# Eight gather slots instead of seven in a fused retention, convolution and expert layer

## The reference

```python
h = rmsnorm(x, g_mix)
q, k, v, g, gb, gc, hc = split(h @ w_in)
o = rms_scale(retention(state, rotary(q), rotary(k), v)) * silu(g)
conv_y, conv_new = short_conv(buf, gc * hc, conv_w)      # y = w0*e[t] + w1*e[t+1] + w2*e[t+2]
x = x + concat([o, gb * conv_y]) @ w_out
# peer(n(x)): per row and head
q = (n(x) @ wq).reshape(T, 8, 2, 128)
v1, i1 = top_k(q[:, :, 0] @ keys1.T, 16);  v2, i2 = top_k(q[:, :, 1] @ keys2.T, 16)
cand = v1[..., :, None] + v2[..., None, :]               # 256 pairs a head
top_s, sel = top_k(cand, 16);  eidx = (i1 * 128 + i2)[sel];  gate = softmax(top_s)
act = gelu(einsum('td,thkd->thk', n(x), u_tab[eidx]))
x = x + einsum('thk,thkd->td', gate * act, v_tab[eidx])
y = rmsnorm(x, g_fin)
```

## Time and profile before

| | |
|---|---|
| median of 3 runs | 3036.95 us (3034.13 to 3040.64) |
| the profiled execution | 3032.31 us, of it the span from first to last instruction 3030.5 us |
| busy shares | PE 75%, DVE 68%, ACT 67%, POOL 41% |
| gathers (software queue) | 1107.36 MB, packet time 88.6% of 16 engines' span |
| other loads and stores (hardware queue) | 116.88 MB, 9.7% |
| HBM traffic | 404 GB/s over the span |

### The profile page before, as it was taken

One profiled execution on the slowest core, in us unless ns is written; L12 is line 12 of the kernel. 1 busy time (PEld: TensorE's weight loads), 2 busy tenths in 40 slices (PEclk: granted clock), 3 DMA queues, 4 the chain that ended last, 5 costly groups with the idle time before them and its releaser, 6 DMA issues.

```text
span 3030.5 us, 36672 instructions
## 1 busy us (share of the span) xinstructions
PE 2286.4 (75%) x12800; PEld 1866.0 (62%) x12800; DVE 2071.6 (68%) x5121; ACT 2024.2 (67%) x3688; POOL 1238.6 (41%) x1060
## 2 busy tenths in 40 slices
PE   9976887787668878876667787888777676666766
PEld 7765776665557766755556665665656555555555
DVE  2467887566688775656888744566588899954454
ACT  1277666668677666686677766667767777676666
POOL 0133433334333333444433444434444444455653
PEclk9988999998888898988988989989878987666666
DMA  7599999999999999999999999999999999999997
GB/s 301 184 421 410 407 410 418 419 420 412 420 421 405 416 420 416 420 407 420 420 417 404 404 419 419 419 417 409 413 420 418 420 412 413 413 419 414 421 420 330
DMA packets 180569, 1226.65 MB, mean 405 GB/s; under 512 B 20736, under 2 KB 21952, under 8 KB 40736
## 3 DMA queue, kind: packets, MB, share of 16 engines
q0 software_dynamic: 152064, 1107.36, 88.6%
q1 hardware_dynamic: 28032, 116.88, 9.7%
q10 hardware_dynamic: 288, 0.07, 0.0%
HBM read 1219.37 MB, written 4.86 MB: 404 GB/s over the span
## 4 chain that ended last, share of the span: by engine, by line
DMA 37%; DVE 23%; PE 22%; ACT 12%; issue 6%; POOL 1%; DVEq 0%; ACTq 0%; POOLq 0%
DMA ring<-in_uv,idx 37%; DVE ring L1467 11%; PE expert_sum L1120 9%; ACT ring L877 5%; PE mm L918 4%; PE mm L927 2%; PE mm L1042 2%; ACT weights L873 2%; PE x_ps L980 2%; DVE pairs_left L1314 1%; ACT dots L864 1%; ACT L864 1%; DVE pairs_left L1402 1%; PE expert_sum L918 1%; POOL ring L662 1%
## 5 line engine op out<-in xcount | busy, mean ns | idle before, releaser
L662 POOL DMA_INDIRECT ring<-in_uv,idx x1056 | 1238.3, 1173 | 1768.3 <-PE expert_sum L1120 1553.9
L1120 PE MATMUL expert_sum<-ident_sb,ring 128*128 128x128 f32 x8448 | 1358.9, 315 | 590.2 <-ACT ring L877 588.5
L1467 DVE CUSTOM_DVE_ANT_0 ring<-ring,xn 128x1024 f32<-128x1024 f32 x1056 | 1286.2, 1222 | 738.1 <-DMA ring<-in_uv,idx 730.5
L1120 PEld LDWEIGHTS expert_sum<-ident_sb,ring 128*128 128x128 f32 x8448 | 1140.5, 163 | 848.3 <-ACT ring L877 781.8
L877 ACT ACTIVATE ring<-ring,weights 128x1024 f32<-128x1024 f32 x1056 | 1213.0, 1149 | 34.4
L864 ACT ACTIVATE dots<-dots 128x1 f32<-128x1 f32 x1056 | 211.6, 200 | 791.2 <-DVE dots L1467 789.2
L873 ACT ACTIVATE weights<-dots,gate 128x1 f32<-128x1 f32 x1056 | 311.1, 295 | 38.1
L918 PE MATMUL mm<-stream,xn_in 128*128 128x256 f32 (+1 forms) x912 | 253.7, 416 | 77.1 <-ACT qkvg L709 61.7
L1042 PE MATMUL mm<-turn,stream 128*128 128x256 f32 (+2 forms) x1024 | 274.1, 396 | 2.8 <-DVE xn_in L1159 2.8
L918 PEld LDWEIGHTS mm<-stream,xn_in 128*128 128x128 f32 (+1 forms) x912 | 164.4, 196 | 116.8 <-ACT qkvg L709 70.5
L927 PE MATMUL mm<-xn_in,stream 128*128 128x256 f32 (+1 forms) x640 | 184.8, 428 | 36.2 <-ACT conv_tmp L700 23.5
(11 more groups left out here) (235 smaller groups left out, 1521.1 us busy)
## 6 DMA issues: line engine op xcount, KB each, us to landing
stream<-in_wq SPq DMA_DIRECT2D x36, 1024.0 KB, 11.8
stream<-in_w_ret SPq DMA_DIRECT2D x26, 1024.0 KB, 9.5
stream<-in_w_conv SPq DMA_DIRECT2D x24, 1024.0 KB, 12.1
ring<-in_uv,idx POOLq DMA_INDIRECT x1056, 12.4
ring<-in_w_ret SPq DMA_DIRECT2D x7, 1024.0 KB, 12.5
x<-in_x SPq DMA_DIRECT2D x8, 512.0 KB, 9.8
w_out_sb<-in_w_out SPq DMA_DIRECT2D x1, 4096.0 KB, 29.1
out_y<-xn SPq DMA_DIRECT2D x8, 512.0 KB, 12.1
```

The source lines that it names most:

```text
L662: pool.indirect_dma_start(ring[:, g % RING, :], None, uv, bass.IndirectOffsetOnAxis(ap=rows, axis=0)).then_inc(landed[g % RING], 16)
L1120: ins = pe.matmul(expert_sum[:, c * P:(c + 1) * P], ring[:, g % RING, D + c * P:D + (c + 1) * P], ident_sb[:, :], is_transpose=True, start ...
L1467: dve.tensor_tensor_reduce(u, u, xn[:, t % 3, :], 1.0, 0.0, ALU.mult, ALU.add, dots[:, g % RING:g % RING + 1]).then_inc(dotted, 1)
```

## The change

- `RING` is 8. All eight blocks of the first group's retention weights are loaded into the ring, and the eighth's two loads into `stream` go. `BUFFERS` stays 3.
- The space for it: `pairs_left` goes. The pairs and the one-hot table stand in `scores`. `best16` replaces in place, with a wait more between FIND_INDEX8 and MATCH_REPLACE8. The one-hot table is made in two halves of 256 with three instructions each.
- ACT's copy of the next scores waits for the whole choice before it (`chosen`) instead of for the last read of the scores.
- `conv_tmp` shrinks to `taps`; the C projection and the filter's result stand in `conv_out`.
- `idx` and `gate` have three places instead of four; from t = 3 on a choice waits until tile t-3's gathers have been weighed.
- `state_s` is `qT`. The sample's state is loaded later and stored earlier, the last group's first query copy waits for that store, and the last group's three tiles take Silu on ACT in place of Tanh on ACT and a multiplication on DVE.
- The rotary table stands in the unused tail of `turn` (for t = 1, of `xn_in`).

```diff
-RING = 7
+RING = 8
...
-    + [(USES[0][use_at(0, "ret", RING, t)][3], 0, "ret", 0, t) for t in GROUPS[0]]
...
-        conv_out = sb("conv_out", [P, CH, wide])
-        conv_tmp = sb("conv_tmp", [P, 2, wide + 4])
+        conv_out = sb("conv_out", [P, CH, wide + 2])
+        taps = sb("taps", [P, wide + 4])
...
-        pairs_left = sb("pairs_left", [P, 2, 2 * NK])
...
-        idx = sb("idx", [P, 4, STEPS], I32)
-        gate = sb("gate", [P, 4, STEPS])
+        idx = sb("idx", [P, 3, STEPS], I32)
+        gate = sb("gate", [P, 3, STEPS])
...
-        state_s = sb("state_s", [P, H, P])
+        state_s = qT[:, :].rearrange("p (h c) -> p h c", h=H)
...
+        hot = scores[:, :, :].rearrange("p s k -> p (s k)")
+        pairs = hot.rearrange("p (i j) -> p i j", i=TOPK)
+        left = xn[:, 2, 0:2 * NK]
...
-                yield base_of(1) + STEPS
-                sp.wait_ge(rotated, 2)
-                sp.dma_start(state_s[:, :, :], ret_state).then_inc(state_in, 16)
+                yield mix_at(SAMPLE) - 20
+                sp.wait_ge(keyed, scores_before(mix_at(SAMPLE)) - 1)
+                sp.dma_start(state_s, ret_state).then_inc(state_in, 16)
...
+            def store_sample_state():
+                yield mix_at(SAMPLE) + 20
+                sp.wait_ge(gated, RANK[SAMPLE] + 1)
+                sp.dma_start(out_ret_s, state_s).then_inc(sample_state_out, 16)
...
                     if kind == "C":
-                        if unit:
-                            act.wait_ge(dve_took, taken(j, q - 1)[1])
-                        act.activation(gate_c[:, 0:width(j)], bank[:, 0:width(j)], ACT.Copy).then_inc(act_took, 1)
+                        wait(act, x1_ready, GROUPS[j][0])
+                        act.activation(conv_out[:, unit // 3, 0:width(j)], bank[:, 0:width(j)], ACT.Copy).then_inc(act_took, 1)
...
+                if j == len(GROUPS) - 1:
+                    g = vg_of(t)[0:n, RET:]
+                    act.activation(g, g, ACT.Silu).then_inc(silu_done, 1)
+                else:
...
+                    if j == len(GROUPS) - 1:
+                        act.wait_ge(sample_state_out, 16)
...
                     if t < SAMPLE:
-                        wait(act, scores_read, pick(h, t) - 1)
+                        act.wait_ge(chosen, pick(h, t))
...
-            def best16(values, indices, s, rest, read=None):
+            def best16(values, indices, s):
                 op(dve.max(values[:, 0:8], s))
                 settle()
                 op(dve.max_index(indices[:, 0:8], values[:, 0:8], s))
...
+                settle()
+                op(dve.match_replace(s, values[:, 0:8], s, LOWEST))
+                settle()
+                op(dve.max(values[:, 8:16], s))
...
                             if s == 0:
                                 dve.wait_ge(keyed_copied, c)
+                                if t > 2:
+                                    dve.wait_ge(weighed, end_of(t - 3))
...
+                        for e in range(2):
+                            part = slice(e * TOPK // 2, (e + 1) * TOPK // 2)
+                            op(dve.tensor_tensor(hot3, bc(iota_sb[0:n, :], 1, TOPK),
+                                                 bc(half_f[0:n, part, :].rearrange("p k s -> p (k s)"), 2, TOPK),
+                                                 ALU.is_equal))
+                            settle()
+                            if e == 0:
+                                yield at + 5
+                            op(dve.tensor_tensor(hot4, hot4, bc(tf, 1, TOPK // 2), ALU.mult))
+                            settle()
+                            op(dve.tensor_reduce(pick_f[0:n, part], hot[0:n].rearrange("p (k b) -> p k b", k=TOPK // 2),
+                                                 AX_X, ALU.add))
+                            settle()
```

More of the change, by code:

```diff
@@ L384, in cs_of @@
         def cs_of(t):
-            return state_s[:, 0:2, :] if t == 1 else cs_sb[:, :, :]
+            tail = (xn_in if t == 1 else turn)[:, 2 * D:2 * D + 2 * P]
+            return tail.rearrange("p (s c) -> p s c", s=2)
         def x_hat_of(t):
@@ L417, in queryT @@
                 return qT[:, s * 2 * P:s * 2 * P + w]
-            return conv_tmp[:, 0, 0:w] if s else qT[:, 0:w]
+            return taps[:, 0:w] if s else qT[:, 0:w]
         def xnT_of_first():
@@ L636, in _ @@
                                *[load_x(t) for t in range(TILES + 1)],
-                               *[load_cs(t) for t in RANK], *[store_y(t) for t in range(TILES + 1)], store_states())
+                               *[load_cs(t) for t in RANK], *[store_y(t) for t in range(TILES + 1)], store_states(),
+                               store_sample_state())
             for slot in range(FIRST, LAST + 1):
                 advance(programs, slot)
-            sp.wait_ge(state_out, 32)
+            sp.wait_ge(state_out, 16)
+            sp.wait_ge(sample_state_out, 16)
             sp.wait_ge(tails_out, 32)
@@ L660, in _ @@
                     pool.wait_ge(projected, use_at(0, "ret", g, 1) + 1)
-                rows = idx[:, 1 if t == SAMPLE else t % 4, k:k + 1]
+                rows = idx[:, 0 if t == SAMPLE else t % 3, k:k + 1]
                 pool.indirect_dma_start(ring[:, g % RING, :], None, uv,
@@ L817, in exponentials @@
                     act.wait_ge(exp_in, pick(last, t) + 1)
-                    g = gate[0:n, t % 4, first * TOPK:(last + 1) * TOPK]
+                    g = gate[0:n, t % 3, first * TOPK:(last + 1) * TOPK]
                     act.activation(g, g, ACT.Exp).then_inc(exp_done, 1)
@@ L873, in _ @@
                 act.activation(w, d, ACT.Copy,
-                               scale=gate[:, 1 if t == SAMPLE else t % 4, k:k + 1]).then_inc(weighed, 1)
+                               scale=gate[:, 0 if t == SAMPLE else t % 3, k:k + 1]).then_inc(weighed, 1)
                 act.wait_ge(weighed, g + 1)
@@ L1380, in choices @@
                                 dve.wait_ge(keyed_copied, c)
-                            best16(tv[:, s, :], ti[:, s, :], scores_of(t, h)[0:n, s, :], left[0:n, s * NK:(s + 1) * NK],
-                                   pick(h, t) if s and t < SAMPLE else None)
+                                if t > 2:
+                                    dve.wait_ge(weighed, end_of(t - 3))
+                            best16(tv[:, s, :], ti[:, s, :], scores_of(t, h)[0:n, s, :])
                         yield at + 2
@@ L1389, in choices @@
                         yield at + 3
-                        best16(bv, bi, pairs[0:n].rearrange("p i j -> p (i j)"), left[0:n])
+                        best16(bv, bi, hot[0:n])
                         settle()
                         yield at + 4
-                        dve.tensor_tensor(gate[0:n, t % 4, h * TOPK:(h + 1) * TOPK], bv,
+                        dve.tensor_tensor(gate[0:n, t % 3, h * TOPK:(h + 1) * TOPK], bv,
                                           bv[:, 0:1].broadcast_to([n, TOPK]), ALU.subtract).then_inc(exp_in, 1)
@@ L1416, in gates @@
                     dve.wait_ge(exp_done, b + 1)
-                    g = gate[0:n, t % 4, first * TOPK:(last + 1) * TOPK].rearrange("p (h k) -> p h k", k=TOPK)
+                    g = gate[0:n, t % 3, first * TOPK:(last + 1) * TOPK].rearrange("p (h k) -> p h k", k=TOPK)
                     op(dve.tensor_reduce(reduced[0:n, 0, 0:heads], g, AX_X, ALU.add))
@@ L1426, in quads @@
                 steps = STEPS // QUADS
+                dve.wait_ge(weighed, end_of(6))
                 dve.wait_ge(chosen, PH * (TILES + 1))
```

81 lines of the change are left out of this document (26 added, 55 removed).

## The result

| kernel | median us | lowest to highest | runs |
|---|---|---|---|
| before | 3034.81 | 3031.39 to 3040.8 | 22 |
| changed | 3040.22 | 3036.64 to 3043.91 | 22 |

The ratio changed to before is 1.0015, 95% interval 1.0009 to 1.0021. That is 0.15% or 4.6 us slower.

A forecast was written before the change was run, and what follows sets the result against it. DMA bytes over rate were taken as the bound, with few per cent left to win. Terms -14 - 2.5 + 1 + 5 + 4 + 1 + 1 = -4.5 us from the median 3036.95 gave 3032.5 us, range 3013 to 3050.

The forecast's parts named there:

- The slot: Gather ring: an eighth slot lengthens the DMA queue's cover from 5.9 to 8.4 us; -14 us.
- three priced dips: Windows of low DMA rate (344, 321, 335 GB/s), one from 700 to 705, priced at 1.8, 1.2 and 2.0 us.
- The choice: DVE: 0.9 us added per choice, mostly hidden by gather waits except from 2400 to 2640; +5 there, +4 elsewhere.
- rival 4: DVE's choice: the new waits cost nothing, 0.3 us less a choice; 3027.5 us, chance 0.07.
- The choice elsewhere: Outside 2400 to 2640: DVE returns some buffers 0.9 us later, giving back a third of the slot's gain; +4 us.
- Rival 2: DVE sets the pace in the choice stretches and the slot gains only 4 us: slower, 3050 us, chance 0.17.
- Rival 3: Gather queue: the eighth buffer only makes gathers queue longer and gains 0; 3046.5 us, chance 0.08.
- Rival 1: Gather ring: the eighth slot closes the dips, worth 28 us; 3016 us, chance 0.22.
- +1 for Silu: Last group's three tiles: extra table loads on ACT hold up gathers' scalings, within the cover; 0 to +8, taken +1 us.
- -2.5 for the bytes: Prologue: one 1 MB load goes, leaving one block less for the saturated part; -2.5 us.
- The start's +1: Gather 7 is issued 2 us later because its buffer holds the eighth weight block; 0 to +2, taken +1 us.
- ACT's wait, +1: ACT's score copy near 434 waits 5.5 us for the choice before, beside PE's own gap; 0 to +5, taken +1 us.

The follow-up runs named there:

- the old choice: Changed kernel with eight slots, but the expert choice and ACT wait of the kernel before, g_fin left out: 3027.8 us, ratio 0.9968 to the kernel before.
- The table of four: Ratios to the kernel before, seven then eight slots: choice of the kernel before 0.9998, 0.9968; changed kernel's choice 1.0060, 1.0022; g_fin left out for all but 1.0060.
- The two kernels with the bf16 table: Changed kernel with a 512-wide bf16 one-hot table, 3031.35 us; the same with the replacement going into idle places, without the three added waits, 3028.22 us.
- the cell 0.9998: Changed kernel with seven gather slots and the choice of the kernel before, g_fin left out: 3036.95 us, ratio 0.9998 to the kernel before.

## Why the prediction was wrong

In the order in which the prediction adds its terms two were mis-sized, each by about 5 us, and both errors made the kernel slower than forecast.

**The slot: forecast -14, measured -9.** The queue did grow by 2.5 us, and that each dip costs less than 2.5 us was read rightly. But one us for each of 14 low slices took for granted that a low slice is a dip that one more gather covers. With the old choice there are still 12 low slices, and of the three priced dips the one at 1305 was not touched. So a price under 2.5 us does not say that the slot covers a dip. That "the 14 low slices rise to 417 or more" was false even where DVE was left alone; by the prediction's own test it was wrong there. The kernel before stood already where another slot brings little (3080.6, 3037.0, 3027.8 us for six, seven, eight).

**The choice: forecast +5 from 2400 to 2640 and +4 elsewhere, measured +14 to +16 in all, of it 10.4 in the stretch.** That the cost would fall where DVE has little waiting left was right. The step that failed is the sentence that the eighth slot lends 2.5 us once: between gathers 784 and 896 it lent nothing. Without the loan the prediction's count is 12.6 - 5.3 = 7.3. Of the other 3 us, 1.5 are seen: the forecast took all that was added to come out of DVE's waits for gathers, but its waits for ACT's copies grew (5.3 us with the old choice, 6.8 with the new, in the stretch; 52.1 and 61.1 over the span). The rest is not accounted for, nor is it shown why those waits grew. The 7.6 us by which the two windows of before and after differ look like the 7.3, and that is luck: by gathers it was 10.2.

The table of four also allows the other order, first the choice at seven slots (19 us) and then the slot (12 to 14 us). The slot by itself then came as forecast, and all of the error is in the choice. The prediction gave 4 us of the slot back for the choice, so the order above is its own; by either order the choice cost more than the 9 us that it had.

The price of the pieces came out as forecast. One sample choice of the changed kernel on DVE (start, us, instruction):

```profile
2524.94 0.42 DVE L1410 TENSOR_REDUCE pick_f<-scores 128x8 f32<-128x256 f32 x1
2525.39 0.42 DVE L1402 TENSOR_TENSOR scores<-iota_sb,half_f 128x256 f32<-128x256 f32 x1
2525.85 0.42 DVE L1408 TENSOR_TENSOR scores<-scores,top_f 128x256 f32<-128x256 f32 x1
...
2537.61 0.41 DVE L1314 FIND_INDEX8 best_i<-best_v,scores 32x8 uint32<-32x256 f32 x1
2538.05 0.08 DVE L1316 MATCH_VALUE_LOAD scores<-best_v,scores 32x8 f32 x1
2538.12 0.40 DVE L1316 MATCH_REPLACE8 scores<-best_v,scores 32x256 f32<-32x256 f32 x1
```

A step of 256 is 0.45 to 0.46 us from start to start. MATCH_VALUE_LOAD starts 0.44 us behind FIND_INDEX8 where it was 0.34: the 0.10 us of a wait. The two kernels with the bf16 table repeat both numbers, 0.44 with the wait and 0.34 without. So the wait that rival 4 took to be free has its price in the rows; in the whole kernel 0.0004 doesn't show it. The Trainium skill ("VectorE: DVE Perf Modes", section on the DRAIN that can't be avoided) says that a semaphore between Vector instructions costs nothing extra, which it measured on copies. The same section says that a following instruction that nothing holds starts earlier, and this is what the rows of this pair show.

**DVE busy for over 228 of 240 us: it was 223.3.** A wrong sign for a right mechanism. Before, DVE was busy for 221.3 us and waited 5.3 us for gathers and 6.0 us for ACT; 7.4 us were gaps between its instructions. Filling the 5.3 us gives 226.6 at most as long as the other two stay. They grew: 223.3 us busy, 6.8 us for ACT and 9.9 us of gaps, while 92 gathers passed instead of 95. The waits for gathers that are gone say that DVE was full, the busy share does not.

**The choice elsewhere: forecast +4, and 4 to 6 are left** of 14 to 16 when 10.4 are taken off. That agrees in size only: no trace locates them, so the mechanism given for the +4 (buffers returned 0.9 us later) is not shown. From 1400 to 1690 the prediction called the cost hidden. DVE's waits in that stretch now:

```profile
DVE top_v L1312 <- ACT scores L811: 12.5, 11, 2.4
DVE ring L1471 <- DMA ring<-in_uv,idx: 11.0, 10, 1.9
```

The 22.2 us for gathers became 11.0: 11 of the 12.6 us came out of waiting, as cover should. It is not all cover: the rate fell from 412 to 408 GB/s (windows, 290 us: 2.8 us), though the old choice with eight slots has 410 there, so that half of it may be nothing. The waits for ACT grew here too, from 9.6 us with the old choice and eight slots to 12.5.

**The small terms.** Gather 7 started 1.55 us later (144.23); what the load less brought was too small to see; ACT stood once, for 6.3 us against 5.5 forecast, and PE's own gap stood beside it as before. Rows of ACT, PE and POOL in the changed kernel:

```profile
441.38 0.38 ACT L811 ACTIVATE scores<-tp 128x256 f32<-128x256 f32 x1 [6.29 <-DVE idx L1413]
...
441.01 2.90 PE L917 MATMUL mm<-stream,xn_in 128*128 128x256 f32 x6 [6.59 <-issue]
...
145.78 1.01 POOL L658 DMA_INDIRECT ring<-in_uv,idx  x1 [3.04 <-PE mm L917]
```

Forecast were +1 for Silu and -2.5 for the bytes; the cell 0.9998, which holds both and the parts put at nothing, has -0.6, by 3 us either way. The start's +1 came with the eighth slot and is not in that cell. ACT's wait, +1, was measured alone as +3, by 4 us either way. None of these terms is refuted and none is confirmed.

**The rivals.** Rival 2 had the mechanism: DVE sets the pace where the choices are dense, and a longer ring does not help there. Its condition, a slot worth less than about 9 us, was met at best at its edge. Its 3050 was too high, since it gave the slot 4 us over the whole span; outside that stretch the slot still brought its 9. Rival 3, slot 0, is refuted by the old choice with eight slots. Rival 1 is refuted by the low slices that stayed.

What stays open: why the eighth slot does not lift the dip at 1305 and the deep slices (398 to 406 GB/s). Where the 4 to 6 us are lost that the medians have over the traces. And the three waits' share of the choice's cost: 0.0004 against intervals of 0.0009 can't tell 1 us from 4.

## What to carry to other kernels

Before paying for a longer ring with instructions of the engine that empties it, ask stage by stage how much waiting that engine has left. What is added beyond that waiting is lost, and the longer ring did not lend it back here. Do not count a dip for the slot by its price alone: of three that all cost less than one gather's time, one stayed as it was. Read fullness from the waits that are gone, not from the busy share, and compare two kernels by the same piece of work, not by the same window of the clock. And look for space that costs no instruction (a type of half the width for small whole numbers, tails that lie idle) before splitting a step in two.

## What the hardware showed that was not expected

- DVE took as long in bf16 as in f32 on these one-hot steps of 512: 692, 688 and 686 ns against 680 ns for the f32 reduction. Half the bytes were no gain in time, only in space.
- Rings of six, seven and eight gathers of 1 MB gave 3080.6, 3037.0 and 3027.8 us: 44 to 50 us for the seventh, 9 for the eighth. The eighth lengthened the median from issue to landing by one gather's 2.5 us.
